# Two output projections of a transformer kernel: eight block products per pair of tiles become seven

## The reference

```
y = concat(o_a, o_b) @ w_out                    # [512, 1024] @ [1024, 1024]
x = x + ga_m * rms_norm(y, g_post_mix)
h = rms_norm(x, g_pre_ffn) * (1 + sc_f) + sh_f
x = x + ga_f * rms_norm(swiglu(h), g_post_ffn)
```

## Time and profile before

| | |
|---|---|
| median of three runs | 2297.11 us |
| span of the profiled execution | 2300.2 us |
| PE busy | 2226.9 us (97%) |
| DVE, ACT, POOL busy | 1108.0, 492.7, 695.8 us |
| `out1`: first product to first product of F0 | 626.31 to 697.74 us |
| `out2`: first product to first product of its feed-forward part | 1813.91 to 1883.42 us |

### The profile page before, as it was taken

How to read it: one execution, slowest core, us unless ns; L and a number is a source line. 1 busy time by engine, 2 the same in 40 slices (tenths; PEclk the granted TensorE clock), 3 DMA queues, 4 the chain that set the end, 5 groups by cost and what they waited for, 6 DMA issues and landing times. The chain is left out here.

```text
span 2300.2 us, 26544 instructions
## 1 busy us (share of the span) xinstructions
PE 2226.9 (97%) x10359; PEld 1740.7 (76%) x10359; DVE 1108.0 (48%) x2054; ACT 492.7 (21%) x1144; POOL 695.8 (30%) x549
## 2 busy tenths in 40 slices
PE   6998989999999999999999999999999999999998
PEld 4443677777677888888888888885557588888887
DVE  5858965655428842345655325441614341112454
ACT  3102332333422000101300011130324440010012
POOL 0000000000104656654465656500000105555642
PEclk8999999999999999999999999999999999999999
DMA  9624345544412462224154412330112122322230
GB/s 346 220 93 125 98 146 183 161 141 122 146 54 93 164 200 75 76 76 124 60 191 153 145 53 76 87 109 24 50 42 74 37 74 74 102 81 62 76 101 37
DMA packets 255639, 250.20 MB, mean 109 GB/s; under 512 B 20098, under 2 KB 207772, under 8 KB 255388
## 3 DMA queue, kind: packets, MB, share of 16 engines
q1 hardware_dynamic: 255080, 248.37, 34.2%
q10 hardware_dynamic: 436, 0.15, 0.0%
HBM read 243.25 MB, written 4.19 MB: 108 GB/s over the span
## 5 line engine op out<-in xcount | busy, mean ns | idle before, releaser
L2167 POOL TENSOR_TENSOR w_sums<-ring 128x512 f32<-128x512 f32 x66 | 90.9, 1378 | 493.2 <-POOLq L1464 301.5
L2195 POOL TENSOR_TENSOR hidden<-rstd,h_act 128x256 f32<-128x256 f32 x66 | 53.5, 811 | 355.2 <-DVE h_act L2371 355.2
L2371 DVE TENSOR_TENSOR h_act<-ps,rstd 128x256 f32<-128x256 f32 x78 | 33.0, 424 | 224.7 <-PE ps L2069 128.1
L2051 PE MATMUL ps<-h_sums,w_sums 128*128 128x256 f32 x528 | 127.4, 382 | 1.2 <-DVE h_sums L2307 0.7
L2063 PE MATMUL ps<-h_sums,w_sums 128*128 128x256 f32 x528 | 125.0, 380 | 2.4 <-DVE rstd L2341 2.4
L2074 PE MATMUL ps<-h_act,w_sums 128*128 128x256 f32 x528 | 124.8, 380 | 1.4 <-DVE h_act L2335 1.4
L2069 PE MATMUL ps<-h_sums,ring 128*128 128x256 f32 x528 | 124.9, 380 | 1.2 <-DVE rstd L2348 1.2
L2017 PE MATMUL ps<-h_act,ring 128*128 128x256 f32 x528 | 125.4, 382 | 0.1
L2057 PE MATMUL ps<-h_act,ring 128*128 128x256 f32 x528 | 124.7, 379 | 0.0
L2025 PE MATMUL ps<-h_act,ring 128*128 128x256 f32 x528 | 124.3, 380 | 0.0
L2341 DVE TENSOR_TENSOR rstd<-ps,h_act 128x256 f32<-128x256 f32 x78 | 33.1, 424 | 182.0 <-PE ps L2051 159.9
(11 more groups left out here) (479 smaller groups left out, 4468.4 us busy)
## 6 DMA issues: line engine op xcount, KB each, us to landing
ring<-in_ffn_w_in SPq DMA_DIRECT2D x66, 1024.0 KB, 7.6
ring<-in_w_mod SPq DMA_DIRECT2D x12, 2048.0 KB, 7.9
ring<-in_w_gate_up SPq DMA_DIRECT2D x22, 1024.0 KB, 7.7
ring<-in_ffn_w_out SPq DMA_DIRECT2D x32, 704.0 KB, 6.1
mod_half<-in_w_ada SPq DMA_DIRECT2D x16, 1024.0 KB, 8.5
ring<-in_w_in SPq DMA_DIRECT2D x6, 2048.0 KB, 8.1
ring<-in_ffn_w_out SPq DMA_DIRECT2D x8, 1408.0 KB, 7.1
ring<-in_w_down SPq DMA_DIRECT2D x16, 704.0 KB, 6.2
```

The lines of the kernel that those rows point to most:

```text
L2051: last = pe.matmul(pb, s2[:, k], F.t2[:, k], start=(k == 0), stop=(k == 3))
L2167: pool.tensor_tensor(s1, a21, a22, ALU.add).then_inc(S["wsum"].sem, 1)
L2195: pool.tensor_tensor(one[:, j], F.gate1[f % 2], F.got21[f % 2], ALU.mult)
```

## The change

Both projections become four units `u`. Unit `u` computes output tiles `u` and `u + 4` for both token halves with seven block products of four 128x128 by 128x256 products each. `A11, A12, A21, A22` are the weight blocks (rows 0 to 511 or 512 to 1023 of `w_out`, tile `u` or `u + 4`); `h11` to `h22` are the input blocks (row half, token half). POOL makes the four weight sums of a unit, DVE the ten input sums once at the start of the stage. Units 0 and 1 run whole; units 2 and 3 first run what the first token half needs. PSUM bank 6 takes the context's sum. `y_add` and `y_square` stay, but ACT now squares from SBUF (except that it copies `kept1` and output 11 out of PSUM). The feed-forward part's first weight sums now wait for the projection's last uses of the same buffers, and both weight halves go back to the ring only after the last product.

```diff
+OUT_PIECES = [(0, 0, SEQ, "set")] + [(k, 0, SEQ, "add") for k in (4, 1, 5)]
+OUT_PIECES += [(2, 0, HALF, "add"), (6, 0, HALF, "add"), (3, 0, HALF, "add"), (7, 0, HALF, "sum")]
+OUT_PIECES += [(6, HALF, SEQ, "add"), (7, HALF, SEQ, "add"), (2, HALF, SEQ, "add"), (3, HALF, SEQ, "sum")]
...
+def out_tensor(K, O, pe):      # each step: 4 products, k = 0 to 3
+    product_1(u): bank a  = A11 h11                 (u >= 2 waits got11 of u - 2)
+    sum_11(u):    bank a += A12 h21                 (waits kept1 of u)
+    product_6(u): bank b  = s2 t2                   (waits wsum 4u + 2; u = 0: each k waits its t2)
+    product_7(u): bank c  = (A11 - A21) h12         (waits wsum 4u + 3)
+    product_5(u): bank b  = s1 t1                   (waits v of u; u = 0: all ten input sums)
+    sum_21(u):    bank c += A22 t4                  (waits w of u)
+    sum_12(u):    bank b += s4 h22                  (waits wsum 4u + 4 and got22 of u)
...
+    product_1(0)
+    product_1(1)
+    sum_11(0)
+    sum_11(1)
+    for u in range(2):
+        product_6(u)
+        context(2 * u)
+        product_7(u)
+        product_5(u)
+        sum_21(u)
+        context(2 * u + 1)
+        sum_12(u)
+    for u in range(2, 4):
+        product_1(u)
+        product_6(u)
+        product_7(u)
+        sum_11(u)
+        sum_21(u)
+    product_5(2)
+    y_sum(K, O.T, pe, 0)
+    product_5(3)
+    sum_12(2)
+    sum_12(3)
+    for half in range(2):
+        K.ring.left_of((O.name, half), S["c12"].sem, S["c12"].base + OUT_UNITS)
+    y_sum(K, O.T, pe, 1)
     x_sum(K, O.T, pe, 0, 0)
-    y_sum(K, O.T, pe, 1)
     x_sum(K, O.T, pe, 0, 1)
-    idle_products(K, pe, 5, 15)
+    idle_products(K, pe, 2, 15)
+
+
+def out_gpsimd(K, O, pool):
+    S = O.S
+    for u in range(OUT_UNITS):
+        a11, a12, a21, a22 = out_weights(K, O, pool, u)
+        s1, s2, s4 = up_sums(O, u)
+        n = 4 * u
+        if u >= 2:
+            S["c12"].wait(pool, u - 1)
+        pool.tensor_tensor(s1, a21, a22, ALU.add).then_inc(S["wsum"].sem, 1)
+        S["wsum"].wait(pool, n + 1)
+        pool.tensor_tensor(s2, s1, a11, ALU.subtract).then_inc(S["wsum"].sem, 1)
+        pool.tensor_tensor(a21, a11, a21, ALU.subtract).then_inc(S["wsum"].sem, 1)
+        S["wsum"].wait(pool, n + 2)
+        pool.tensor_tensor(s4, a12, s2, ALU.subtract).then_inc(S["wsum"].sem, 1)
...
+def out_vector(K, O, dve):
...
     if O.context:
         coefs_1(K, dve, O.done)
...
+    for k in range(4):
+        dve.tensor_tensor(O.h12[:, k], O.h22[:, k], O.h12[:, k], ALU.subtract).then_inc(S["hsum"].sem, 1)
+        S["hsum"].wait(dve, 2 * k + 1)
+        dve.tensor_tensor(O.t2[:, k], O.h12[:, k], O.h11[:, k], ALU.add).then_inc(S["hsum"].sem, 1)
+    S["hsum"].wait(dve, 8)
+    dve.tensor_tensor(O.t1, O.h22, O.t2, ALU.subtract).then_inc(S["hsum"].sem, 1)
+    dve.tensor_tensor(O.t4, O.h21, O.t2, ALU.subtract).then_inc(S["hsum"].sem, 1)
+    for u in range(2):
+        give_v(u)
+        give_w(u)
+        give_22(u)
+        if u:
+            y_add(K, T, dve, 1)
+        give_21(u)
+        give_12(u)
+    context(0, 1, 2)
+    give_v(2)
+    y_add(K, T, dve, 2)
+    give_w(2)
+    y_add(K, T, dve, 3)
+    context(3, 4)
+    give_21(2)
+    context(5, 6)
+    give_v(3)
+    y_add(K, T, dve, 4)
+    give_w(3)
+    y_add(K, T, dve, 5)
+    context(7)
+    give_21(3)
+    y_add(K, T, dve, 6)
     if O.context:
         dve.wait_ge(K.restored, 16)
...
+    give_22(2)
+    x_turned(K, T, dve, 0, 0)
+    give_22(3)
+    x_turned(K, T, dve, 0, 1)
+    y_add(K, T, dve, 8)
+    give_12(2)
+    x_new(K, T, dve, 0, 0)
+    give_12(3)
+    y_add(K, T, dve, 9)
+    y_add(K, T, dve, 10)
+    x_new(K, T, dve, 0, 1)
+    x_new(K, T, dve, 0, 2)
+    tail_vector(K, T, dve)
...
 def fast_gpsimd(K, F, pool):
...
+    if F.sums_left is not None:
+        F.sums_left.wait(pool, OUT_UNITS - 1)
     up_weight_sums(0)
...
+    if F.sums_left is not None:
+        F.sums_left.wait(pool, OUT_UNITS)
     up_weight_sums(1)
```

More of the change, by code:

```diff
@@ new lines, in product_1, with sum_11 @@
+    def product_1(u):
+        a11 = out_weights(K, O, pe, u)[0]
+        pa = fast_banks(K, u)[0]
+        if u >= 2:
+            S["got11"].wait(pe, u - 1)
+        for k in range(4):
+            last = pe.matmul(pa, a11[:, k], O.h11[:, k], start=(k == 0), stop=(k == 3))
+        last.then_inc(S["p1"].sem, 1)
+    def sum_11(u):
+        a12 = out_weights(K, O, pe, u)[1]
+        pa = fast_banks(K, u)[0]
+        S["kept1"].wait(pe, u + 1)
+        for k in range(4):
+            last = pe.matmul(pa, a12[:, k], O.h21[:, k], start=False, stop=(k == 3), skip_group_check=True)
+        last.then_inc(S["c11"].sem, 1)
@@ new lines, in product_6, with product_7 @@
+    def product_6(u):
+        pb, s2 = fast_banks(K, u)[1], up_sums(O, u)[1]
+        S["wsum"].wait(pe, 4 * u + 2)
+        if u >= 2:
+            S["got12"].wait(pe, u - 1)
+        for k in range(4):
+            if u == 0:
+                S["hsum"].wait(pe, 2 * k + 2)
+            last = pe.matmul(pb, s2[:, k], O.t2[:, k], start=(k == 0), stop=(k == 3))
+        last.then_inc(S["p6"].sem, 1)
+    def product_7(u):
+        a21 = out_weights(K, O, pe, u)[2]
+        pc = fast_banks(K, u)[2]
+        S["wsum"].wait(pe, 4 * u + 3)
+        if u >= 2:
+            S["got21"].wait(pe, u - 1)
+        for k in range(4):
+            last = pe.matmul(pc, a21[:, k], O.h12[:, k], start=(k == 0), stop=(k == 3))
+        last.then_inc(S["p7"].sem, 1)
@@ new lines, in product_5, with sum_21 @@
+    def product_5(u):
+        pb, s1 = fast_banks(K, u)[1], up_sums(O, u)[0]
+        if u == 0:
+            S["hsum"].wait(pe, 10)
+        S["v"].wait(pe, u + 1)
+        for k in range(4):
+            last = pe.matmul(pb, s1[:, k], O.t1[:, k], start=(k == 0), stop=(k == 3))
+        last.then_inc(S["p5"].sem, 1)
+    def sum_21(u):
+        a22 = out_weights(K, O, pe, u)[3]
+        pc = fast_banks(K, u)[2]
+        S["w"].wait(pe, u + 1)
+        for k in range(4):
+            last = pe.matmul(pc, a22[:, k], O.t4[:, k], start=False, stop=(k == 3), skip_group_check=True)
+        last.then_inc(S["c21"].sem, 1)
@@ L1869, in out_tensor, with sum_12, context @@
+    def sum_12(u):
+        pb, s4 = fast_banks(K, u)[1], up_sums(O, u)[2]
+        S["wsum"].wait(pe, 4 * u + 4)
+        S["got22"].wait(pe, u + 1)
+        for k in range(4):
+            last = pe.matmul(pb, s4[:, k], O.h22[:, k], start=False, stop=(k == 3), skip_group_check=True)
+        last.then_inc(S["c12"].sem, 1)
+    def context(i):
+        if O.context:
             for k in (2 * i, 2 * i + 1):
@@ L1890, in out_scalar @@
     if O.context:
-        squares(0, 1)
         act.wait_ge(O.done, 2)
[L1893 to L1906, removed]
@@ L1907, in out_scalar @@
-    tail_scalar(K, O.T, act)
-def out_vector(K, O, dve):
+    piece(0, "got12", 1)
+    piece(1, "got12", 1)
+    squares(6, 7)
+    if O.context:
+        act.wait_ge(O.sums, KT)
+        act.activation(O.rstd, O.total, ACT.Ln, bias=K.eps[:, 0:1], scale=1.0 / D).then_inc(O.log, 1)
+        act.wait_ge(O.log, 1)
+        act.activation(O.rstd, O.rstd, ACT.Exp, scale=-0.5).then_inc(O.rstd_done, 1)
+    piece(2, "got12", 2)
+    piece(3, "got12", 2)
+    keep_1(2)
+    give_11(2)
+    piece(4, "got11", 3)
@@ L1912, in out_vector @@
     if O.context:
         coefs_1(K, dve, O.done)
[L1914 to L1925, removed]
```

160 lines of the change are left out of this document (121 added, 39 removed).

## The result

| | before | after |
|---|---|---|
| median, 20 runs each, side by side | 2302.05 us (2296.42 to 2311.03) | 2311.65 us (2306.12 to 2317.63) |
| after / before | | 1.0042, 95% interval 1.0031 to 1.0054 |
| span of the profiled execution | 2300.2 us | 2315.6 us |
| first product to F0's first product, first projection | 71.43 us | 78.48 us |
| the same, second projection | 69.51 us | 71.75 us |

The change makes the kernel 0.42% slower, where +3.9 us (+0.17%) was forecast, and 2311.65 us lies outside the range of 2287 to 2309. In the two profiled executions the two projections with their tails account for 7.05 + 2.24 = 9.3 us, the medians for 9.6.

What follows compares the result with a forecast made beforehand. PE, busy 2226.9 of 2300.2 us, was taken as the bound. First projection -6.8 + 2.7 + 1.3 + 6.1 = +3.3, second -6.8 + 1.3 + 6.1 = +0.6; together +3.9 on 2297.1 gives 2301.0 us, range 2287 to 2309.

Steps and rivals of the forecast that it cites:

- The seven block products save what was forecast: Both projections: 112 products take 48.35 us instead of 55.2, saving 6.8 us each, 13.6 in all.
- product_6(0) waits for `t2`: First projection's start: `t2`'s last block is ready at 10.9 us where product_6 wants it at 8.2, 2.7 late.
- the middle of the first projection: Context operations ahead of `give_v(2)` meet POOL's sums for unit 3; 1.3 us lost, nothing in the second projection.
- A: The forecast itself: the lock delays starts and tails, +3.9 us to 2301.0, alone 2296 to 2306; chance 0.55.
- B: Lock hardly on the path, starts and middle free, tails 13.6 us: 10.2 faster, 2286.9; chance 0.2.
- C: Tails too stay at 11.95 us: 13.6 faster, 2283.5; chance 0.07.
- The weights come back later: Ring returns half 0 only after the last product, two loads asked for at once: no cost, up to 2 us.
- The lock: POOL and DVE with two SBUF inputs each pass a port instruction by instruction, the loser fully blocked; bandwidth is not split.
- Start, 14.0 in the first projection and 13.2 in the second: DVE's eight small additions alternate with POOL's sums, 1.3 us each; start 2.7 us late in first projection, 1.3 in second.
- rival D: Clock falls in stalled places, 1.5 us each, where late in the tails, plus a longer start: 2309.5; chance 0.1.
- Tail, 18.1: From PE's last product: POOL's eight feed-forward sums hold seven DVE operations, 18.1 us instead of 11.95, 6.1 lost per projection.
- +2 of the start: Upper end for the starts, if every POOL sum stands fully ahead of DVE and none is issued early: 2 us more.

Runs made afterwards that it cites:

- e5_start_split: Kernel after, but of unit 0's four POOL weight sums only the first two run at once, the others behind DVE's eight small additions; 1.0000 of before.
- e1_late_sums: Kernel after, but POOL's first four feed-forward sums wait for half 0's three `x_normed`, the next four for all ten input sums; 0.9990 of before.
- e3_before_sums_in_tail: Kernel before, but POOL makes the feed-forward part's first eight weight sums only after the projection's last product, in both projections; 1.0052 of before.
- e6_both: Kernel after with both the late feed-forward sums and the split of unit 0's first weight sums; 0.9980 of before.
- e2_start_wait: Kernel after, but POOL's first sum of a projection waits for DVE's eighth input sum; 1.0033 of before.
- e4_start_filler: Kernel after with twelve unread products in front of product_6(0); 1.0042 of before.
- e7_reorder: e6_both with the tail's DVE and ACT order changed and eight unread products instead of fifteen; 0.9981 of before.
- e8_f1_too: e7_reorder, but POOL's first sums at F1 also wait for `x_normed`, the next ones for all ten input sums; 0.9963 of before.

## Why the prediction was wrong

**Right in kind.** The seven block products save what was forecast: in the second projection, from the first product to the end of the last, e5_start_split takes 50.8 us where the kernel before takes 57.6, both with the short stretch at the low clock and without a wait, 6.7 less (6.8 forecast). product_6(0) waits for `t2` and the middle of the first projection costs 1.33 us (1.3 forecast). POOL's sums stand in the tail and hold DVE one instruction at a time. The direction is right, too: A's path, and neither B nor C, whose tails of 13.6 and 11.95 were not there. The weights come back later, as forecast without cost: they are asked for at 689.90 and 690.32 in the first projection, and no wait of PE behind either projection ends with such a load. The lock, argued from the earlier trace rows and read in the Trainium skill's SBUF — State Buffer, section "Who interferes with whom", was put to the test by e1_late_sums and e3_before_sums_in_tail: with POOL elsewhere the tail's DVE instructions have their free durations, with POOL beside them those with two SBUF operands are held until the sum under way has ended. The traces agree with that rule.

**The failed step: the size of what the holds cost.** I wrote +3.9 us; the traces have 9.3, so 5.4 more.

- *Start, 14.0 in the first projection and 13.2 in the second.* I priced each alternation at 1.3 us ("1.27 + 0.42 less the free starts and the early issue"). It is 1.38 and 1.49 in turn, start to start 2.82 for a pair. The eight take 0.7 us longer: 14.72 instead of 14.0 (e1_late_sums) and 13.97 instead of 13.2. Term too small by 0.7 in each stage.
- *The clock in the first start.* I had the fall as something that "each of the three stalled places can have" in rival D, and not in the forecast. In the kernel after it came, and p5(0) is 16.41 where e1_late_sums, with the same two waits and no fall, has 14.72: 1.7 us. These are the only two executions with that wait in full, so how often the fall comes is open.
- *Tail, 18.1.* Measured 19.07 and 18.86. `y_sum` waits 5.0 us as forecast (4.9). What came late is `x_sum` of half 1: 15.31 us from the end of the products in the second tail (14.8 said): seven operations, "each held 0.6 to 0.9 us, 5.4 in all", were held 0.7 to 1.1 each, 6.3 in all (against the durations in e6_both), and 0.5 of that reaches PE. And it is 3.55 us from there to F0's first product, not 3.3. In the first tail it is 15.62: `x_sum` of half 0 took 5.41 us at the low clock, the unread products came later for it, and they stood in front. I had reckoned that a fall which is over by then is free, because ACT and DVE have slack; it bit in PE's own queue instead, for 0.3 us.
- Together 0.7 + 1.7 + 1.0 and 0.8 + 0.8 make 5.0; 0.4 stays unassigned, which is what rounding of the steps and the restarts after a wait (1.97 instead of 1.89 us) may hold.

**The base.** The range was laid on 2297.11 us, a median of three. The median of the 20 runs is 2302.05, 4.9 us higher. Of the 10.6 us between 2301.0 and 2311.65, nearly half comes from there. The range as a difference ended at +12 us and the measured difference is +9.6 (interval of the ratio, +7 to +12); the absolute time is outside because I trusted three runs to 3 us, with one of the three at 2307.28 on the table.

**Rival D**, 2309.5, came nearest in time, partly by its own means. Its price of 1.5 us for a fall was met in the first start (1.7). Its "+2 of the start" does not follow from its own terms: 5.9 + 8 x 1.13 + 1.4 is 16.3, which is 3.5 more than the 12.8 of the forecast. In the tails the clock was back before `x_sum` of half 1, where D needed it low, and the start was 0.7 over the forecast. What else brings the measured time near it is the base.

## What to carry to other kernels

Before moving work onto an engine that shares a path with another, list where their instructions with two SBUF operands now coincide; a short one is held for the whole of the long one (0.42 becomes 1.4 us), so a chain of many short operations loses most. Ask of each such sum who needs it and when: two of four at once and the rest behind the chain gave 7.3 us in the traces here (5.6 without the fall of the clock), without any work removed. A change that saves the bottleneck engine 13.6 us can lose all of it in the two chains at its ends, and each can be tried by itself: here that gave back 17.3 us in the traces. And work that once filled a gap, like the 15 unread products, is worth another look when the chain beside it has moved.

## What was not expected of the hardware

**Where the clock falls.** Each of the eight tails with the 5 us wait for `y_add` (after, e2_start_wait, e4_start_filler, e5_start_split) has a stretch at 0.50 that begins inside that wait; so have both of e3_before_sums_in_tail, at or soon after the end of a wait of 2.9 us. The eight tails of e1_late_sums, e6_both, e7_reorder and e8_f1_too, with waits of 1.85 us or less, have none. In the kernel after, the stretch of the first tail is about twice as long as that of the second, and the same wait of 0.78 + 2.11 us at the first start had one in one kernel and none in another. What decides it within such a wait was not tried.

**A DVE operation with one tensor operand was held as well.** `tensor_scalar` (128x512, L564) reads one tensor and a column of coefficients. In e1_late_sums the group of four that writes `tmp` has a median of 474 ns, and the one that met POOL's sum, at 709.51, took 1490:

```profile
L564 DVE TENSOR_SCALAR tmp<-ring,cc x4: 474/474/1490, 709.5 to 781.6; 128x512 f32<-128x512 f32 x4
```

POOL's timeline in the same execution:

```profile
709.27 1.45 POOL L2398 TENSOR_TENSOR w_sums<-ring,w_sums 128x512 f32<-128x512 f32 x1
```

The sum ends at 710.72, the operation at 711.00. "One with at most one does not", as the prediction has it, is thus too narrow. The Trainium skill's SBUF — State Buffer, "Who interferes with whom", excepts the instructions in a two-port mode and names `tensor_scalar` among those that can enter one, and this row is what that exception would give.
